# One-core hybrid attention layer: output weights split by SyncE and GpSimd, forget logits and memory values in fewer matmuls, sums of squares on turned rows, diagonals one unit ahead

## What is computed

```python
h = rmsnorm(x, norm_w)                      # x: 1024 tokens x 1024
proj = h @ w_in                             # 4616 columns, float32
sb_q, sb_k, sb_v, fx_q, fx_k, fx_v, f_logit, m_q, gate = split(proj)
sb_out = stick_breaking_attention(sb_q, sb_k, sb_v)      # 8 heads of 64
log_f_cum = cumsum(log_sigmoid(f_logit + b_forget))      # 8 heads
fx_out = forgetting_attention(fx_q, fx_k, fx_v, log_f_cum)   # 8 heads
m_k, m_v = split(rmsnorm(mem, mem_norm_w) @ w_mem_kv)    # 256 memory rows
m_out = memory_attention(m_q, m_k, m_v)                  # 4 heads
y = concat(sb_out, fx_out, m_out)           # 20 heads x 64 = 1280
y = rmsnorm_per_head(y) * out_norm_w * silu(gate)
out = rmsnorm(x + y @ w_out, final_norm_w)
```

## Time and profile before

| | us |
|---|---|
| median of 3 runs | 878.24 (877.83 to 881.8) |
| the profiled execution, its time | 882.52 |
| its span, first to last instruction | 880.8 |
| PE busy | 834.1 |
| DVE busy | 572.2 |
| ACT busy | 480.7 |
| POOL busy | 255.1 |
| mean granted clock of TensorE | 0.987 |

### The profile page before, as it was taken

One profiled execution on the slowest core, in us unless ns is written; L12 is line 12 of the kernel. 1 busy time (PEld: TensorE's weight loads), 2 busy tenths in 40 slices (PEclk: granted clock), 3 DMA queues, 4 the chain that ended last, 5 costly groups with the idle time before them and its releaser, 6 DMA issues.

```text
span 880.8 us, 12476 instructions
## 1 busy us (share of the span) xinstructions
PE 834.1 (95%) x4384; PEld 696.0 (79%) x4384; DVE 572.2 (65%) x1187; ACT 480.7 (55%) x932; POOL 255.1 (29%) x377
## 2 busy tenths in 40 slices
PE   8998978898999999999999999999998998999996
PEld 8667757787888888888888888887887886878885
DVE  5635535565667786676778667677755666675475
ACT  5744647674576455567555556655555683443221
POOL 1133543423124522412453222244423112310000
PEclk9999989999999999999999999999999999999999
DMA  7024883420300320030222003030301288152432
GB/s 289 25 73 124 278 274 137 162 79 24 96 25 25 96 96 25 25 96 25 63 58 96 24 25 101 23 93 26 120 25 45 76 295 301 52 174 86 168 119 96
DMA packets 33373, 88.96 MB, mean 101 GB/s; under 512 B 3352, under 2 KB 11544, under 8 KB 32288
## 3 DMA queue, kind: packets, MB, share of 16 engines
q1 hardware_dynamic: 28992, 72.44, 25.1%
q10 hardware_dynamic: 4320, 15.73, 4.8%
HBM read 57.72 MB, written 21.53 MB: 90 GB/s over the span
## 4 chain that ended last, share of the span: by engine, by line
PE 77%; DVE 9%; ACT 6%; issue 5%; DMA 2%; POOL 1%; ACTq 0%; DVEq 0%; POOLq 0%; SPq 0%
PE banks L645 12%; PE banks L647 12%; PE banks L646 12%; PE banks L687 10%; PE banks L801 7%; PE banks L818 4%; PE banks L819 4%; PE banks L787 4%; PE banks L788 4%; DVE work L1428 2%; PE banks L862 2%; PE banks L839 2%; PE banks L753 2%; DMA wo_dram<-work 1%; DVE pT L1465 1%
## 5 line engine op out<-in xcount | busy, mean ns | idle before, releaser
L645 PE MATMUL banks<-hT,w_parts 128*128 128x512 f32 x576 | 242.8, 422 | 8.0 <-DVE fx_heads L1359 3.7
L647 PE MATMUL banks<-hT,w_parts 128*128 128x512 f32 x576 | 227.7, 395 | 0.0
L646 PE MATMUL banks<-hT,w_parts 128*128 128x512 f32 x576 | 227.5, 395 | 0.0
L999 ACT ACTIVATE pT<-banks 128x512 fp32r<-128x512 f32 x208 | 97.0, 498 | 150.1 <-PE banks L801 149.4
L1465 DVE TENSOR_TENSOR pT<-banks,pT 128x512 fp32r<-128x512 f32 x208 | 111.7, 563 | 98.0 <-ACT pT L999 97.9
L1207 POOL TENSOR_TENSOR w_parts<-w_raw,w_parts 128x1024 fp32r<-128x1024 f32 x40 | 96.4, 2409 | 175.7 <-ACT w_parts L913 175.7
L645 PEld LDWEIGHTS banks<-hT,w_parts 128*128 128x128 f32 x576 | 109.9, 191 | 24.9 <-DVE fx_heads L1359 4.4
L647 PEld LDWEIGHTS banks<-hT,w_parts 128*128 128x128 f32 x576 | 109.3, 190 | 24.9
L646 PEld LDWEIGHTS banks<-hT,w_parts 128*128 128x128 f32 x576 | 110.2, 191 | 12.9
L801 PE MATMUL banks<-ident,work 128*128 128x128 f32 x640 | 94.6, 274 | 0.0
L1215 POOL TENSOR_SCALAR_AFFINE_SELECT work<-work 128x128 f32<-128x128 f32 x64 | 35.1, 548 | 202.2 <-ACT work L979 201.7
(11 more groups left out here) (212 smaller groups left out, 1396.4 us busy)
## 6 DMA issues: line engine op xcount, KB each, us to landing
w_raw<-in_w_tiles SPq DMA_DIRECT2D x40, 512.0 KB, 3.3
wo_dram<-work ACTq DMA_DIRECT2D x16, 512.0 KB, 3.7
hT<-wo_dram SPq DMA_DIRECT2D x16, 512.0 KB, 8.3
work<-in_w_out ACTq DMA_DIRECT2D x8, 512.0 KB, 3.8
fx_heads<-fx_heads SPq DMA_DIRECT2D x8, 512.0 KB, 7.6
negL<-negL_dram SPq DMA_DIRECT2D x8, 512.0 KB, 6.7
yT_dram<-silu SPq DMA_DIRECT2D x8, 512.0 KB, 5.0
sb_heads<-sb_heads SPq DMA_DIRECT2D x8, 512.0 KB, 7.4
```

The source lines that it names most:

```text
L645: pe.matmul(o, w[:, 0, k, :], hT[:, 0, k, tok], start=(k == 0), stop=False)
L646: pe.matmul(o, w[:, 0, k, :], hT[:, 1, k, tok], start=False, stop=False)
L647: mm = pe.matmul(o, w[:, 1, k, :], hT[:, 0, k, tok], start=False, stop=(k == KT - 1))
L999: act.activation(pT[:, n % 3, 0, cols], banks[:, T_BANK + n % 2, cols], ACT.Copy).then_inc(t_hi, 1)
```

## The change

Six edits, made together.

1. Output weights: SyncE issues the loads and stores, GpSimd does both the copy (a `tensor_scalar` by 1.0) and the subtraction; there are six pairs of buffers and a new list of ticks (load, split; the stores two ticks after the split).
2. Forget logits: upper weights four times and lower weights once stand side by side (40 columns), so two matmuls do what three did; DVE adds the two results (one more small operation for each half).
3. Memory values: computed like the memory keys (24 matmuls of 256 columns for each piece) and turned afterwards (`MT`, four transposes in ticks 2 and 3).
4. Sums of squares: TensorE turns `yT` (four transposes), ScalarE squares in PSUM (`square_rows`), DVE sums over 64 columns (`reduce_sum`).
5. GpSimd writes the diagonal of unit i+1 in tick i.
6. Order: on ScalarE and DVE the parts of `T_AT` come before the small pieces; `forget_end` and the last `split_next` of `FIRST` move into tick 1; a one-column Exp after the Ln loads the Exp table; the values of phase 2 are turned at tick 28 (was 22).

```diff
@@ small_pieces
-    out = []
+    out = [Small("MT", c, None, 2 + c) for c in range(2)]
...
-            tick = max(READ_TICK[q] + 1, UNITS * (p.of - 1) + 6)
+            tick = max(READ_TICK[q] + 1, UNITS * (p.of - 1) + (12 if p.of == 2 else 6))
...
-W_OUT_LOAD = [(0, 1), (2, 0), (4, 2), (7, 1), (9, 0), (11, 2), (14, 1), (16, 0), (23, 0), (30, 0)]
+W_OUT_LOAD = [(0, 3, 0), (0, 3, 1), (2, 5, 2), (3, 6, 3), (5, 8, 4), (6, 9, 5), (10, 13, 2), (12, 15, 4), (14, 17, 5), (16, 25, 3)]
...
@@ sync
+            def store_w_out(j):
+                pair = W_OUT_LOAD[j][2]
+                sp.wait_ge(wo_lo, j + 1)
+                sp.dma_start(wo_dram[j, 0, :, :], wo_rows[pair][1]).then_inc(wo_out[pair], 16)
+                sp.dma_start(wo_dram[j, 1, :, :], wo_rows[pair][0]).then_inc(wo_out[pair], 16)
...
@@ tensor, forget_logits
-                    pe.matmul(o, forget_hi[:, f], hT[:, 0, k, tok], start=(k == 0), stop=False)
-                    pe.matmul(o, forget_hi[:, f], hT[:, 1, k, tok], start=False, stop=False)
-                    mm = pe.matmul(o, forget_lo[:, f], hT[:, 0, k, tok], start=False, stop=(k == KT - 1))
+                    w = forget_w[:, k, :, :].rearrange("p x f -> p (x f)")
+                    pe.matmul(o, w, hT[:, 0, k, tok], start=(k == 0), stop=False)
+                    mm = pe.matmul(o, w, hT[:, 1, k, tok], start=False, stop=(k == KT - 1))
@@ tensor, small
-                    pe.wait_ge(sq_done, 2 * p.of + TURN[p.c] + 1)
-                    pe.wait_ge(ones_done, 1)
+                    pe.wait_ge(o_read, 4 * p.of + 2 + TURN[p.c] + 1)
                     for b in range(4):
-                        mm = pe.matmul(o[:, 2 * b:2 * b + 2], o_tmp[:, b * P:(b + 1) * P], pair_ones[:, :], start=True, stop=True)
+                        t = 4 * p.c + b
+                        mm = pe.transpose(o[:, b * P:(b + 1) * P], yT[:, t * P:(t + 1) * P], ident[:, :])
@@ scalar
-            def square_half(g):
-                t = UNIT[4 * g]
-                act.wait_ge(o_read, g + 1)
-                act.activation(o_tmp[:, :], yT[:, t.c * CW:(t.c + 1) * CW], ACT.Square).then_inc(sq_done, 1)
+            def square_rows(n):
+                act.wait_ge(small_ready, n + 1)
+                act.activation(banks[:, SMALL_BANK, :], banks[:, SMALL_BANK, :], ACT.Square).then_inc(sq_done, 1)
@@ gpsimd
+            def split_w_out(j):
+                raw, hi = wo_rows[W_OUT_LOAD[j][2]]
+                pool.wait_ge(wo_in[W_OUT_LOAD[j][2]], 16 * wo_turn(j))
+                pool.tensor_scalar(hi.bitcast(F32R), raw, 1.0, None, ALU.mult).then_inc(wo_hi, 1)
                 pool.wait_ge(wo_hi, j + 1)
                 pool.tensor_tensor(raw.bitcast(F32R), raw, hi, ALU.subtract).then_inc(wo_lo, 1)
...
-                elif i < N_UNITS and UNIT[i].kind == "fx":
-                    diagonal(i)
+                if i + 1 < N_UNITS and UNIT[i + 1].kind == "fx":
+                    diagonal(i + 1)
@@ vector, finish_small, N1
-                    dve.wait_ge(small_ready, n + 1)
+                    dve.wait_ge(sq_done, 2 * p.of + TURN[p.c] + 1)
+                    link(dve.reduce_sum(sums, src.rearrange("p (n d) -> p n d", d=HD), AX_X))
```

More of the change, by code:

```diff
@@ L184 @@
 PIECE, PH_PIECES, N_TILES = all_pieces()
-HI_BEFORE = firsts(0 if p.what in ("V", "F", "O") else 1 for p in PIECE)
+HI_BEFORE = firsts(0 if p.what in ("V", "F", "O", "memV") else 1 for p in PIECE)
 def piece_of(what, c, of):
@@ L569, in _ @@
                 if q == len(FIRST) - 1:
-                    sp.wait_ge(f_scan, 1)
-                    sp.dma_start(negL_dram[:, :], f_m).then_inc(negL_out, 16)
+                    load_w_out(0)
+                    load_w_out(1)
                 piece_end(q)
+            sp.wait_ge(f_scan, 1)
+            sp.dma_start(negL_dram[:, :], f_m).then_inc(negL_out, 16)
             for i in range(X0):
+                for j, (load, split, _) in enumerate(W_OUT_LOAD):
+                    if i == split + 2:
+                        store_w_out(j)
+                    if i == load and j > 1:
+                        load_w_out(j)
                 for q in DONE[i]:
@@ L579, in _ @@
                     sp.wait_ge(negL_out, 16)
-                    sp.wait_ge(wo_out[2], 32 * sum(1 for _, pair in W_OUT_LOAD if pair == 2))
+                    sp.wait_ge(wo_out[0], 32 * W_OUT_TURNS[0])
                     load_negL(0, 0)
@@ L916, in evacuate @@
                 p = PIECE[q]
-                if p.what in ("V", "F", "O"):
+                if p.what in ("V", "F", "O", "memV"):
                     return
@@ L922, in evacuate @@
                 if p.what == "Q":
+                    if p.of == 2 and p.c == 0:
+                        for i in (4, 5):
+                            act.wait_ge(wo_out[i], 32 * W_OUT_TURNS[i])
                     d = q_of(region_of(p.of))
@@ L935, in evacuate @@
                     else:
-                        act.wait_ge(wo_out[2], 32 * sum(1 for _, pair in W_OUT_LOAD if pair == 2))
+                        act.wait_ge(wo_out[0], 32 * W_OUT_TURNS[0])
                     ins = act.activation(gate_of(p.of)[:, cols], src, ACT.Sigmoid)
@@ L1291, in _ @@
                         split_lo(PIECE[q].tile + 2)
-                for j, (tick, _) in enumerate(W_OUT_LOAD):
-                    if i == tick + 3:
-                        w_out_lo(j)
+                for j, (_, split, _) in enumerate(W_OUT_LOAD):
+                    if i == split:
+                        split_w_out(j)
         @block.vector
@@ L1337, in evacuate @@
                     dve.wait_ge(piece_ready, q + 1)
-                    if p.of == 3:
-                        dve.wait_ge(wo_out[0], 32 * sum(1 for _, pair in W_OUT_LOAD if pair == 0))
+                    if p.of < 4 and p.c == 0:
+                        place = 1 if p.of == 2 else 5
+                        dve.wait_ge(wo_out[place], 32 * W_OUT_TURNS[place])
                     dve.tensor_copy(v_raw(p.of, p.c), src).then_inc(piece_done, 1)
+                    return
+                if p.what == "memV":
+                    dve.wait_ge(piece_ready, q + 1)
+                    dve.tensor_copy(mem_v_raw[p.c], src[:, 0:MEM]).then_inc(piece_done, 1)
                     return
@@ L1593, in _ @@
                     forget_begin()
-                if PIECE[q].what == "memV" and PIECE[q].c == 0:
-                    forget_end()
             for i in range(N_TICKS):
@@ L1602, in _ @@
                     mem_max(i)
+                if i == 1:
+                    forget_end()
                 for q in READ[i]:
@@ L1606, in _ @@
                     y_lo(n)
+                for n in T_AT[i]:
+                    lower_part(n)
                 for n in SMALL_AT[i]:
```

172 lines of the change are left out of this document (77 added, 95 removed).

## The result

Before 878.9 us (median of 4 runs, 877.8 to 881.8), after 867.35 us (median of 4, 866.5 to 868.3): ratio 0.986, 95% interval 0.983 to 0.988. So 11.5 us came where 23 were forecast. The first table shows where they went: the starts of the phases, read from the first scores matmul of each in the two traces. (The traces are of single executions, of 882.5 and 867.8 us, so their gain of 14.8 us is larger than that of the medians.)

What follows compares the result with a forecast made beforehand. TensorE's work plus its idle time was taken as the bound (busy 834.1 of 880.8 us). Terms 5.5 + 7.5 + 5.1 - 1.9 + 7.3 = 23.5, rounded to 23, gave 859.5 us from the profiled 882.5, 855 from the median; range 847 to 866.

Steps and rivals of the forecast that it cites:

- I take 1.2, half of the two-input operation: Output weights: GpSimd's 128x1024 copy taken as 1.2 us, between bounds of 0.6 and 2.41; the edit gains 7.5 us.
- rival 1: Memory phases: GpSimd becomes the bound once the cover is used up, costing 8 to 10 us: 864; chance 0.17.
- 2 to 3 us: Memory phases: GpSimd's queue done at 127, PE at tick 23 near 129.5, so 2 to 3 us of cover.
- 1.0 charged: Tick 19: small DVE operations held by busy GpSimd for up to 2.4 us; 1.0 us charged.
- 5.1 gained, 1.9 lost: Norm edit: 15 places gain 0.34 us of PE each, 5.1; (b) and the memory phases' losses sum to -1.9.
- (b): Second memory phase, tick 23 before the spread of tick 25: longer norm chain loses 1.2 us, reordered parts return 0.8.
- Stores at tick 28, 0.5 charged: First fox phase's values, turned at tick 28: last stores land near 148, needed near 146.5; 0.5 us charged.
- Diagonals, 7.3: Fox scores: earlier diagonals gain 6.2 us in first and last fox phases, 1.1 at two other waits; 7.3 total.
- Rival 2: Fox phases: the diagonal's wait only moves to unit 9, 2 x 3.1 us not gained: 861; chance 0.13.
- Prelude, first projection at 77.8: Before the first memory phase: PE idles until weights are split at 77.8; gain 1.7 us, not 8.1.
- Rival 3: Norm chain shows everywhere: DVE's added sums delay 18 places by 0.7 us each, 5.1 lost: 873; chance 0.08.
- Rival 5: Memory phases: SyncE's queue lands weight loads late behind stores, about 24 us lost: 879 or more; chance 0.04.

Runs made afterwards that it cites:

- copy_tc: The changed kernel with GpSimd's copy of each output tile as a plain tensor_copy instead of a multiplication by 1.0; 857.7 us, ratio 0.974.
- n1_psum: The changed kernel with the norm's sums of squares and a copy of the row sums in PSUM; 867.0 us, ratio 0.985.
- spread_late: The changed kernel with norm sums in PSUM, output tiles split later, and the spread of norm scales behind upper parts and output copy on ScalarE; 856.9 us, 0.973.
- tc_late: The changed kernel with GpSimd's plain copy and the spread of norm scales moved behind the upper parts on ScalarE; 861.2 us, ratio 0.978.
- copy_act: The changed kernel with the ten output-weight copies on ScalarE ahead of the exponentials, subtractions still on GpSimd; 874.2 us, ratio 0.993.
- a_old_norm: The changed kernel with the norm edit undone: ScalarE squares to o_tmp, matmuls with pair_ones sum; 871.2 us, ratio 0.988.

## Why the prediction was right or wrong

- **Output weights, the copy: "I take 1.2, half of the two-input operation".** This is the step that failed, by a size: the copy as written takes 2.78 us, above the 2.41 that was set as its upper bound. The mechanism was laid out and held as rival 1: once its cover is used up, GpSimd's queue shows. With 2.78 the prediction's own count gives 9 x 1.58 - 2.5 = 11.7 us. Measured against copy_tc, the second memory phase lost 11.0 and both memory phases together 8.1, since the change had the shorter scan in the first. Rival 1's 864 was short because it stopped at 2.4. At 1.04 us a copy the kernel comes to 857.7 and the edit's own part to 22.7 - 14.0 = 8.7, of 7.5 forecast.
- **The cover, "2 to 3 us".** It was worked out too small. By the prediction's own terms 5.5 + 7.5 = 13.0 us are gained before tick 23, which puts it at 144.8 - 13.0 = 131.8 and not at 129.5 (copy_tc has it at 133.2). The cover is then near 5 us and the count gives 9.4.
- **The whole sum.** In copy_tc it comes to 22.7 us of 23, and that is partly luck. Diagonals and output weights brought more than forecast (9.9 and 8.7, of 7.3 and 7.5), the norm less, and if the parts add up, which no run shows, 1.8 are left for the prelude and ticks 0 to 4, of 5.5.
- **What was argued for 1.2**, that one operand costs half of two, is true of the plain copy (1.04 of 2.43) and untrue of a multiplication by a constant. By the Trainium skill (GPSIMD Engine Reference, section 4.1 Engine selection) one-input work goes at roughly line rate: the trace agrees for the copy and not for the other. The factor of about two that the section gives for two-input work is against VectorE, so it did not support "half" on one engine.
- **"1.0 charged" for VectorE held by GpSimd.** The mechanism was right and the size too small for the instructions: ticks 19 and 23 show 3.9 and 2.3 us above the 0.17 of each. With the short copy 1.5 us are left at tick 19 and none at 23. What they cost the whole kernel is not shown, since n1_psum only moved them.
- **Norm: 5.1 gained, 1.9 lost (0.5 of it for the stores), 3.7 net.** Measured 2.3, with the slow copies in. The place named in (b), the spread at tick 25, is where a wait arose: PE's wait at tick 26 is 3.5 us in copy_tc, 1.29 before, and spread_late removes it in its plan. How much of it the norm edit makes is not shown, as said above. The sum in (b), 0.6 + 0.7 - 0.45, is 0.85 and not 1.2. The 5.1 were too many: after the memory phases 1.8 are gained. In the first fox phase tick 10 takes 6.4 us in the change and 5.3 without the edit.
- **Stores at tick 28, 0.5 charged.** This was too small. In the change ScalarE waits 4.55 us and PE 1.62 of them; in copy_tc PE waits 1.39, and in tc_late 3.77, its longest wait in the memory phases.
- **Diagonals, 7.3.** 9.9: the 1.0 taken off twice for a late transposed part did not come (4.2 and 4.0 gained, 3.1 each forecast), and the middle phases gave 2.5, not 1.1. Rival 2 did not happen: nothing waits for unit 9's diagonal.
- **Prelude, first projection at 77.8.** The phase began at 76.7, and tick 4 came 5.3 us sooner (86.4 for 91.7), 5.5 forecast. But 2.8 of that hang on an order that changes from kernel to kernel: in copy_tc tick 4 comes at 89.2. In eight of the eleven kernels with the scan in tick 1 it takes 4.4 us, so the 0.4 charged for it was luck in the change and too small in most others (last section).
- **Rival 3** (the sums show everywhere) fell; the sum itself takes 0.685 us, 0.7 forecast. **Rival 5** (SyncE) fell as a cause, though copy_act shows its lateness where it is not covered.

Left open: why the norm edit brings only 1.8 us after the memory phases. Tick 10 of the fox phases is a part of it. The last phase is 1.1 us longer in the change than in a_old_norm, but 0.6 us shorter in copy_tc, whose norm chain is the same, so that part is not shown to be the edit's. Open too is why tc_late is 3.5 us behind copy_tc: 2.1 of them lie in the first memory phase (41.7 against 39.6), where the lists of both are the same and the scan starts 0.6 us later.

## What to carry to other kernels

A copy that also rounds should be written as a copy: on GpSimd the same bytes through `tensor_scalar` cost 2.7 times as much (2.78 and 1.04 us). When work goes to an idle engine, count its queue over the stretch in question, not over the span (32% in all, 86% in the first memory phase here), and put an unknown operation's upper bound above the nearest row, not at it. A wait that is removed shows the next late thing: after each fix read what is queued behind the same place.

## What the runs showed of the hardware

- GpSimd, 128x1024, 4-byte floats in SBUF: copy 1.04 us, subtraction of two tiles 2.39, multiplication by a constant 2.78 (ten of ten between 2.77 and 2.78).
- VectorE and GpSimd, both at work in SBUF, keep each other out for a whole instruction, and who starts first decides. The scan of the forget prefix takes 2.28 us in the change, where it starts at 82.22 and GpSimd's subtraction at 82.99 takes 3.69; in copy_tc GpSimd starts first, at 82.77:
```profile
82.77 2.40 POOL L1212 TENSOR_TENSOR w_parts<-w_raw,w_parts 128x1024 fp32r<-128x1024 f32 x1 [4.58 <-ACT w_parts L937]
85.11 3.03 POOL L1249 CAST negL<-silu 128x1024 fp32r<-128x1024 f32 x1
```
```profile
82.90 4.41 DVE L1542 TENSOR_TENSOR_SCAN work<-work 8x1024 f32<-8x1024 f32 x1
```
  The scan then takes 4.41, and tick 4 comes at 89.2 instead of 86.4. At the end of the second memory phase this lead is gone where GpSimd's copies are slow (171.3 us in the change, 171.8 and 172.0 in a_old_norm and n1_psum with the long scan). The Trainium skill (SBUF — State Buffer, section Who interferes with whom) says that issue order decides who blocks, which these rows agree with.
- The same section of the Trainium skill says that single-operand operations of VectorE can be caught too, in their two-port modes; the 2.24 and 1.18 us of L1317 and L1318 in n1_psum agree.
